# The last scaling of a hybrid decoder block: one VectorE instruction per tile, or one on ScalarE and one on GpSimd

## The reference, cut to what matters

```python
def rmsnorm(x, g):
    xf = x.astype(jnp.float32)
    y = xf * lax.rsqrt(jnp.mean(xf * xf, axis=-1, keepdims=True) + EPS)
    return (y * g.astype(jnp.float32)).astype(x.dtype)
...
    y = jnp.zeros((N, D), h.dtype).at[tok_sorted].add(y_disp[dest] * w_sorted[:, None].astype(h.dtype))
...
        x = x + hierarchical_moe(rmsnorm(x, g_moe[l]), w_router_group[l], b_router_group[l], ...)
    return rmsnorm(x, g_final)
```

## Time and profile before

| | |
|---|---|
| median of three runs | 2985.01 us (2983.37 to 2987.5) |
| the profiled execution | 2986.91 us, of which the span of the profile is 2985.1 us |
| busy over the span | PE 2697.3 us, DVE 1607.6, ACT 1276.0, Pool 603.4 |
| DMA | 507.59 MB, mean 170 GB/s |
| final stage | first load issued at 2912.28 us, last instruction of DVE ends at 2982.04 |
| in it | DVE 61.73 us busy, ACT 24.38, Pool 0, PE 0 |

### The profile page before, as it was taken

One profiled execution on the slowest core, in us unless ns is written; L12 is line 12 of the kernel. 1 busy time (PEld: TensorE's weight loads), 2 busy tenths in 40 slices (PEclk: granted clock), 3 DMA queues, 4 the chain that ended last, 5 costly groups with the idle time before them and its releaser, 6 DMA issues. The chain is left out here.

```text
span 2985.1 us, 37254 instructions
## 1 busy us (share of the span) xinstructions
PE 2697.3 (90%) x12695; PEld 2064.1 (69%) x12695; DVE 1607.6 (54%) x2121; ACT 1276.0 (43%) x2112; POOL 603.4 (20%) x702
## 2 busy tenths in 40 slices
PE   6999999999988999999799996899829999999980
PEld 5777787777765666667699995777726776766650
DVE  3624525424336655665544443554566677777658
ACT  4334334333325667667311113553305555655543
POOL 0000000000014555654222220000012222334420
PEclk9999999999998999999899997999959999999995
DMA  4263353453540211112453434121346999999988
GB/s 164 81 188 125 118 164 121 139 177 130 163 113 27 58 37 37 39 36 80 143 155 116 116 119 173 64 106 64 134 200 237 359 366 359 361 364 365 348 311 345
DMA packets 168270, 507.59 MB, mean 170 GB/s; under 512 B 40384, under 2 KB 69312, under 8 KB 140000
## 3 DMA queue, kind: packets, MB, share of 16 engines
q1 hardware_dynamic: 149728, 472.59, 46.1%
q0 software_dynamic: 18432, 33.60, 3.1%
HBM read 431.19 MB, written 108.33 MB: 181 GB/s over the span
## 5 line engine op out<-in xcount | busy, mean ns | idle before, releaser
L486 DVE TENSOR_TENSOR fr_wl<-fr_raw,fr_wh 128x1024 fp32r<-128x1024 f32 x128 | 156.7, 1224 | 469.9 <-ACT fr_wh L357 469.5
L2336 DVE TENSOR_TENSOR ex_gl<-ba_raw,ex_gh 128x2048 fp32r<-128x2048 f32 x128 | 290.2, 2290 | 145.1 <-ACT ex_gh L2267 145.0
L357 ACT CAST fr_wh<-fr_raw 128x1024 fp32r<-128x1024 f32 x128 | 134.0, 1047 | 491.7 <-PE fr_acc L281 491.7
L2267 ACT CAST ex_gh<-ba_raw 128x2048 fp32r<-128x2048 f32 x128 | 240.6, 1907 | 86.0 <-DMA ba_raw<-in_w_exp 43.8
L908 ACT ACTIVATE at_pf<-at_psS 128x512 f32<-128x512 f32 (+1 forms) x320 | 178.4, 559 | 167.6 <-PE at_psS L793 84.2
L1026 POOL TENSOR_TENSOR at_pl<-at_pf,at_ph 128x512 fp32r<-128x512 f32 (+1 forms) x160 | 195.3, 1220 | 259.3 <-ACT at_ph L909 258.8
L2231 PE MATMUL ex_psY<-ba_raw,ex_hT 128*128 128x512 f32 x512 | 231.7, 595 | 7.6 <-issue 6.3
L2210 PE MATMUL ex_psG<-ex_gh,ex_xh 128*128 128x512 f32 x512 | 225.2, 440 | 2.8 <-DVE ex_hm L2347 1.4
L982 DVE TENSOR_TENSOR at_pl<-at_pf,at_ph 128x512 fp32r<-128x512 f32 (+2 forms) x160 | 145.5, 913 | 140.2 <-ACT at_ph L909 137.0
L943 DVE TENSOR_REDUCE at_nm<-at_psA 128x1 f32<-128x512 f32 (+2 forms) x320 | 182.8, 604 | 63.5 <-PE at_psA L827 43.2
L2212 PE MATMUL ex_psG<-ex_gh,ex_xl 128*128 128x512 f32 x512 | 201.0, 393 | 0.0
(11 more groups left out here) (323 smaller groups left out, 6047.1 us busy)
## 6 DMA issues: line engine op xcount, KB each, us to landing
ba_raw<-in_w_exp SPq DMA_DIRECT2D x192, 1024.0 KB, 16.1
fr_raw<-in_w_slabs SPq DMA_DIRECT2D x128, 512.0 KB, 4.2
gates_d<-fr_gst SPq DMA_DIRECT2D x64, 256.0 KB, 4.6
mx_gt<-gates_d SPq DMA_DIRECT2D x64, 256.0 KB, 5.1
cb_ys<-y_d SPq DMA_DIRECT2D x16, 1024.0 KB, 11.2
xa_xe<-x_d SPq DMA_DIRECT2D x18, 512.0 KB, 5.8
mx_xr<-in_x SPq DMA_DIRECT2D x8, 1024.0 KB, 7.1
x_d<-mx_xo SPq DMA_DIRECT2D x8, 1024.0 KB, 5.0
```

The source lines that it names most:

```text
L2267: nc.scalar.copy(gh[:, s, i], raw[:, r, i, :].rearrange("p (k n) -> p k n", k=KD // 2)).then_inc(w_hi, 1)
L2336: V.tensor_tensor(gl[:, s, i], raw[:, r, i, :].rearrange("p (k n) -> p k n", k=KD // 2), gh[:, s, i], ALU.subtract).then_inc(w_lo, 1)
```

## The change

ACT now multiplies the tile of x with the reciprocal of its root and writes the result slot, and Pool multiplies that slot with g_final in place. DVE keeps the two adds and the reciprocal. ACT does the scaling of tile i-1 after the square and the root of tile i, and it is ACT that now waits for the store of the tile three before. A new semaphore `scaled` goes from ACT to Pool; `done` now comes from Pool. Pool waits once for g_final. ACT's wait on `rcp_done` ahead of the square falls away. SP's program is the same.

```diff
--- before.py
+++ after.py
@@ -2396,6 +2396,7 @@
         stored = [s_.sem(f"stored{i}") for i in range(3)]
         g_in, eps_set, first_added, added, sq_done, rms_done, rcp_done, done = (s_.sem(n) for n in (
             "g_in", "eps_set", "first_added", "added", "sq_done", "rms_done", "rcp_done", "done"))
+        scaled = s_.sem("scaled")
         y_rows = y_d.rearrange("(i p a) d -> i p (a d)", p=P, a=2)
         block = ctx.enter_context(nc.Block())
 
@@ -2439,34 +2440,41 @@
                 dve.wait_ge(first_added, i + 1)
                 V.scalar_tensor_tensor(x_tile(i), ys[:, i % R, 1, :], wts[:, i, 1:2], x_tile(i), ALU.mult, ALU.add).then_inc(added, 1)
 
-            def norm(i):
+            def inverse(i):
                 dve.wait_ge(rms_done, i + 1)
                 V.reciprocal(st[:, i % 2, 2:3], st[:, i % 2, 1:2]).then_inc(rcp_done, 1)
-                dve.wait_ge(rcp_done, i + 1)
-                if i >= 3:
-
-                    dve.wait_ge(stored[i % 3], 16 * (i // 3))
-                if i == 0:
-                    dve.wait_ge(g_in, 16)
-                V.scalar_tensor_tensor(yo[:, i % 3, :], x_tile(i), st[:, i % 2, 2:3], gb[:], ALU.mult, ALU.mult).then_inc(done, 1)
 
             add(0)
             for i in range(NT):
                 if i + 1 < NT:
                     add(i + 1)
-                norm(i)
+                inverse(i)
+
+        @block.gpsimd
+        def _(pool):
+            pool.wait_ge(g_in, 16)
+            for i in range(NT):
+                pool.wait_ge(scaled, i + 1)
+                nc.gpsimd.tensor_tensor(yo[:, i % 3, :], yo[:, i % 3, :], gb[:], ALU.mult).then_inc(done, 1)
 
         @block.scalar
         def _(act):
+            def scale(i):
+                act.wait_ge(rcp_done, i + 1)
+                if i >= 3:
+
+                    act.wait_ge(stored[i % 3], 16 * (i // 3))
+                nc.scalar.mul(yo[:, i % 3, :], x_tile(i), st[:, i % 2, 2:3]).then_inc(scaled, 1)
+
             act.wait_ge(eps_set, 1)
             for i in range(NT):
                 act.wait_ge(added, i + 1)
-                if i >= 2:
-
-                    act.wait_ge(rcp_done, i - 1)
                 nc.scalar.activation(sq[:], x_tile(i), ACT.Square, accum_out=st[:, i % 2, 0:1]).then_inc(sq_done, 1)
                 act.wait_ge(sq_done, i + 1)
                 nc.scalar.activation(st[:, i % 2, 1:2], st[:, i % 2, 0:1], ACT.Sqrt, bias=eps[:], scale=1.0 / D).then_inc(rms_done, 1)
+                if i > 0:
+                    scale(i - 1)
+            scale(NT - 1)
 
 
 def program(nc, a, out):
```

## The result

The changed kernel takes 3002.21 us (median of 5, 2997.63 to 3003.77) against 2986.21 us for the kernel before, now with five runs (2983.37 to 2987.5). The ratio is 1.0050, 95% interval 1.0037 to 1.0063. The forecast was 3001.3, slower, in a range from 2996.5 to 3008.

What follows compares the result with a forecast made beforehand. DVE was taken to bound the final stage, the DMA engines close behind. Insertions less removed scalings (+11.9 us) and a longer tail (+4.4) gave +16.3, for the median 3001.3 us, +0.55%; range 2996.5 to 3008.

Steps and rivals of the forecast that it cites:

- What bounds the stage: Final stage: DVE bounds at 3.91 us a tile; the DMA engines come next at 3.70 us.
- What is removed: DVE's scaling in the final stage: 1.20 us a tile, leaving 2.71 us; fourteen scalings make 16.8 us.
- ACT's price: ACT's added 128x1024 multiplication with a per-partition pointer: 1.15 us each, between 1.05 and 1.45.
- Pool's price: Pool's added 128x1024 multiplication of two SBUF tensors: 2.39 us, taken from a flat subtraction.
- Where the two meet: DVE's adds and Pool's multiplication exclude each other on SBUF: one insertion of 2.05 us a tile, making 4.76 us.
- The open point: Whether DVE's scalar_tensor_tensor adds contend with Pool like plain tensor_tensor; if not, the tile falls back to 3.70 us.
- The sum: Finish of tile 15's adds moves +11.9 us, 14 x (2.05 - 1.20); with the tail, together +16.3 us.
- The tail: From the end of tile 15's adds to the span's end: 10.50 us instead of 6.07, +4.4.
- The waits behind: SP's loads queued behind stores, and ACT's scaling waiting for stores, 13.0 us within 14.3: neither binds.
- Not slower: Rival: DVE's adds don't contend with Pool; tile 3.70 us, -2.9 us, no change that can be told; chance 0.07.
- The faster rival: No contention and stores never hold ACT, so the DMA engines bound the stage: about -8 us; chance 0.03.
- The costlier hand-over: Rival: Pool's multiplication slower than a subtraction, 2.63 to 3.2 us, adding +4 to +13 us; chance 0.10.

Runs made afterwards that it cites:

- e1: Changed kernel without Pool's multiplication, so g_final is left out and ACT's scaling releases the store; stage 66.94 us against 72.82 before, ratio to before 0.9984.
- e2: Changed kernel with Pool filling an unread scratch tile instead of multiplying (g_final left out), reading nothing from SBUF; stage 70.74 us, ratio to before 0.9983.
- e8: Changed kernel with Pool multiplying in place by the constant 1, one input instead of two (g_final left out); stage 73.32 us, executed once.
- e6: Changed kernel without Pool's block: ACT multiplies with the reciprocal, DVE with g_final; stage 70.89 us against 72.82 before, executed once.
- e3: Changed kernel with the first add's result in PSUM, where the second add reads it; stage 74.06 us, ratio to before 0.9997.
- e4: Kernel before with the first add's result in PSUM and nothing else; stage 72.81 us against 72.82, executed once.
- e5: Changed kernel with tiles 14 and 15 each scaled by one DVE instruction; stage 82.21 us against 86.41 changed, ratio to before 1.0043.
- e7: Changed kernel with the first add's result in PSUM and the last two tiles scaled on DVE; stage 69.77 us, ratio to before 0.9979.
- e10: e7 plus a semaphore of its own for DVE's two results, so DVE skips a wait for Pool; stage 70.27 us, ratio to before 1.0008.

## Why the prediction was right, point by point

**What bounds the stage.** Right: DVE before, with the DMA engines' 3.70 us next. e1, e2 and e8, in which DVE's adds are nearly or wholly free, all come to 3.70 us a tile, with ACT waiting for stores. That nothing could bring the tile under 3.70 us holds for the steady part only: in e1 tiles 2 to 6 take 2.57 us each, while the first six loads are ahead.

**What is removed.** Mis-sized. The prediction took 3.91 - 1.20 = 2.71 us for a tile without its scaling. The changed kernel has 2.57: in the timeline above an unblocked tile lasts from 2944.66, the end of one second add, to 2947.23, the end of the next. With the scaling went also the wait for the reciprocal, 0.12 us, which the prediction left in; e6 shows it by itself. Removed are 1.34 us a tile.

**ACT's price.** 1.15 forecast, 1.132 measured. No table load was added (one of 1283 ns, as before).

The Trainium skill ("ScalarE: Activation LUTs", What ACT_TABLE_LOAD costs) gives 186 ns, 93 for a pointer and 0.833 ns an element, an estimate of 1132 ns; the row agrees to the nanosecond.

**Pool's price.** 2.39 forecast from a subtraction, 2.34 measured for the multiplication unblocked.

**Where the two meet.** Right in kind and near in size: 2.05 forecast, and 3.25 - 1.28, some 1.98, measured; 14 insertions forecast and 14 found. Three tiles take 13.69 us (2944.66 to 2958.35), 4.56 each, instead of 4.76. The open point, whether scalar_tensor_tensor is held up like the plain form, is settled by the changed kernel itself, and its condition by e2 (Pool's fill, which reads nothing, holds up no add), e3 (the add with one tensor from SBUF is never held up) and e4 (no other effect of PSUM).

The rule of the Trainium skill that the prediction weighed ("SBUF — State Buffer", Who interferes with whom) held for two-input instructions on both sides. For a Pool instruction with one input, e8 shows far less than an exclusive lock over its length, in one profile; there the measurement decides, and the cause stays open.

**The sum.** The finish of tile 15's adds moved by 9.4 us, from 66.74 to 76.13 after the stage's start, by the measured terms 14 x (1.98 - 1.34) = 9.0; forecast +11.9. Of the 2.5 us between the two, 14 x 0.14 = 2.0 are the removed time and 14 x 0.07 = 1.0 the insertion, less some 0.4 that the measured terms fall short, partly because long first adds take 3.29 us and the very first 3.41. The tail is 10.28 us against 6.08, +4.2; forecast +4.4, and e5 confirms it. The whole is 13.6 against 16.3. That the median of the first five runs lay 16.0 over before, next to the forecast, is partly luck: the errors of the sum go the same way, and the scatter of whole executions made up for them; the second set gave 3001.54 against 2988.43, 13.1.

**The waits behind.** Right: neither loads nor the ring of outputs bind in the changed kernel. Output lands in a median of 3.1 us against 8.2 before:

```profile
out<-cb_yo SPq DMA_DIRECT2D x16, 512.0 KB, 3.1
```

**The rivals.** "Not slower" asked for adds that never contend; e2 is that case, and it was priced at 2.9 us under before: the stage is 2.1 under. The faster rival needed a ring that never holds ACT; in e1 and e2 it holds ACT for 12.7 and 13.0 us. The costlier hand-over did not come.

## What to carry to other kernels

Before work is moved from DVE to Pool, look at what both read: if DVE's instructions and Pool's each take two tensors from SBUF, their times nearly add, whatever the busy shares say; an input in PSUM frees DVE's instruction. When such a kernel lands on a number that another limit also gives, as e3 does with 3.69 us, look at who waits for whom before naming the limit. Price the removed instruction with its wait on what fed it, and price the tail apart, since a faster tile and a longer last chain have different signs. When only a small stage is edited, measure the stage from its own first instruction: here it repeated to 0.15 us in two profiles of the changed kernel, where whole executions scatter by several.

## What the runs showed of the hardware

- A two-input multiplication of 128x1024 on Pool takes 2.34 us, one with a constant 2.76 us at the shortest (e8): fewer inputs were not faster.
- That one-input instruction let most two-input adds of DVE pass beside it (1.28 us), where the two-input one held 14 of 32 to about 3.25.
- A fill of 128x2688 on Pool (2.34 us) never held up DVE (e2).
- An add with two tensors from SBUF that was taken up 0.13 us ahead of Pool's multiplication went through (1.29 us, e7); taken up 0.01 or 0.04 us ahead it was held up (3.44 in e3, 3.48 in e10).
- A scalar_tensor_tensor with its result or one input in PSUM takes 1.28 us, as from SBUF (e4).
